# VectorE's order per job in the MLP of a hybrid decoder block: the job's weight panels split first, its slot evicted second

## What is computed

```
v = rms_norm(h, g_ffn[i])
up = causal_dwconv(v @ w_up[i], w_conv_ffn[i], b_conv_ffn[i])   # w_up 1024 x 6144, 3 taps along the sequence
gate = up[..., :D_FF]                                           # D_FF = 3072
val = up[..., D_FF:]
h = h + (jax.nn.gelu(gate) * val) @ w_down[i]                   # w_down 3072 x 1024
```

## Time and profile before

| | |
|---|---|
| median of 3 runs | 2380.67 us (2378.57 to 2381.3) |
| profiled execution, span | 2378.7 us (its own time beside the span is not listed) |
| TensorE busy | 2294.0 us, 96% of the span, 9968 matmuls |
| VectorE busy | 1281.4 us, 54% |
| ScalarE busy | 814.1 us, 34% |
| DMA | 142.47 MB, mean 60 GB/s |
| chain that ended last | PE 86%, DVE 5%, ACT 5%, issue 2%, DMA 1% |

### The profile page before, as it was taken

How to read it: one execution, slowest core, us unless ns; L and a number is a source line. 1 busy time by engine, 2 the same in 40 slices (tenths; PEclk the granted TensorE clock), 3 DMA queues, 4 the chain that set the end, 5 groups by cost and what they waited for, 6 DMA issues and landing times.

```text
span 2378.7 us, 27030 instructions
## 1 busy us (share of the span) xinstructions
PE 2294.0 (96%) x9968; PEld 1882.6 (79%) x9968; DVE 1281.4 (54%) x1532; ACT 814.1 (34%) x971; POOL 0.2 (0%) x4
## 2 busy tenths in 40 slices
PE   7999999999999999999889999999999999999995
PEld 5787888888888888887767778888888888888784
DVE  6774466524653355545677735654255624554445
ACT  5663333202331133333545624332133302333432
POOL 0000000000000000000000000000000000000000
PEclk9999999999999999999999999999999999999997
DMA  3113111111111111123121031111111111111123
GB/s 126 45 45 121 39 54 54 45 54 45 53 46 50 49 46 53 45 82 114 54 98 50 31 133 45 53 45 53 45 53 46 50 49 45 54 45 54 54 66 110
DMA packets 69715, 142.47 MB, mean 60 GB/s; under 512 B 7504, under 2 KB 7632, under 8 KB 69584
## 3 DMA queue, kind: packets, MB, share of 16 engines
q1 hardware_dynamic: 69584, 140.68, 18.3%
HBM read 132.26 MB, written 8.39 MB: 59 GB/s over the span
## 4 chain that ended last, share of the span: by engine, by line
PE 86%; DVE 5%; ACT 5%; issue 2%; DMA 1%; SPq 0%; ACTq 0%; DVEq 0%
PE slot L355 85%; DMA raw<-panels 1%; DVE H L770 1%; DVE H L834 1%; PE slot L388 1%; ACT L481 1%; PE slot L404 1%; DVE wlo L671 0%; ACT whi L472 0%; ACT L567 0%; DVE H L832 0%; ACT H L567 0%; DVE H L789 0%; ACT Uhi L504 0%; ACT H L569 0%
## 5 line engine op out<-in xcount | busy, mean ns | idle before, releaser
L355 PE MATMUL slot<-Uhi,whi 128*128 128x512 f32 x2176 | 677.1, 392 | 29.1 <-DVE wlo L671 21.6
L355 PE MATMUL slot<-Ulo,whi 128*128 128x512 f32 x2176 | 672.9, 390 | 0.0
L355 PE MATMUL slot<-Uhi,wlo 128*128 128x512 f32 x2176 | 672.0, 390 | 0.0
L472 ACT ACTIVATE whi<-raw 128x512 fp32r<-128x512 f32 x428 | 247.3, 623 | 979.4 <-PE slot L355 926.8
L355 PEld LDWEIGHTS slot<-Uhi,whi 128*128 128x128 f32 x2176 | 409.6, 189 | 122.6 <-DVE Ulo L704 22.6
L355 PEld LDWEIGHTS slot<-Ulo,whi 128*128 128x128 f32 x2176 | 410.4, 189 | 86.0
L355 PEld LDWEIGHTS slot<-Uhi,wlo 128*128 128x128 f32 x2176 | 410.2, 189 | 85.7
L355 PE MATMUL slot<-Ylo,whi 128*128 128x512 f32 x1024 | 316.7, 390 | 0.0
L671 DVE TENSOR_TENSOR wlo<-raw,whi 128x512 fp32r<-128x512 f32 x428 | 276.3, 686 | 29.9 <-ACT whi L472 26.9
L901 DVE TENSOR_TENSOR H<-slot,H 128x1024 f32<-128x1024 f32 x48 | 58.8, 1225 | 334.1 <-PE slot L355 334.1
L680 DVE TENSOR_TENSOR WG<-slot,RS 128x1024 f32<-128x1024 f32 x72 | 88.2, 1225 | 268.4 <-PE slot L355 267.9
(11 more groups left out here) (146 smaller groups left out, 1463.7 us busy)
## 6 DMA issues: line engine op xcount, KB each, us to landing
raw<-panels SPq DMA_DIRECT2D x432, 256.0 KB, 2.7
XN<-xT SPq DMA_DIRECT2D x8, 1024.0 KB, 10.2
H<-xT SPq DMA_DIRECT2D x8, 1024.0 KB, 10.0
outT<-H SPq DMA_DIRECT2D x16, 512.0 KB, 3.0
WG<-pT SPq DMA_DIRECT2D x2, 512.0 KB, 4.8
WV<-pT SPq DMA_DIRECT2D x2, 512.0 KB, 6.3
par<-parameters SPq DMA_DIRECT2D x1, 136.0 KB, 2.2
```

What stands on the lines that cost most here:

```text
L355: mm = pe.matmul(ps[:, t], stat[n % RING][:, w], mov[:, t], start=first and k == 0 and i == 0, stop=last and k == ks - 1 and i == len(pass ...
L472: nc.scalar.activation(whi[n % RING][:], raw[n % RING][:], ACT.Copy).then_inc(panel_hi, 1)
```

## The change

In the MLP VectorE's `refill` moves ahead of the eviction of the same job. For gate and val jobs it moves ahead of `scaled_out` (and so ahead of `f_lo(j - 1)` and the halo copy); for down jobs it moves ahead of the addition to H, but stays behind the wait for the job. The same instructions run, with the same waits and the same semaphores. ScalarE, TensorE and SyncE are unchanged.

```diff
                         v.tensor_copy(work[:, 0:HALO_FFN], halo_c[:, i:i + HALO_FFN])
                         if (j, stream) == (0, 0):
                             dve.wait_ge(dve_chain, ffn_scale)
+                        refill(jj, bp_c)
                         scaled_out(b, jj, work[:, HALO_FFN:HALO_FFN + BLOCK], bj, bs)
                         if stream == 0 and j:
                             f_lo(j - 1)
                         v.tensor_copy(halo_c[:, i:i + HALO_FFN], work[:, BLOCK:BLOCK + HALO_FFN]).then_inc(ready, 1)
-                        refill(jj, bp_c)
                         dve.wait_ge(summed, pairs + j + 1)
...
                     for m in range(DT):
                         jj = JOBS[("down", 0, m)]
                         dve.wait_ge(jobs_done, bj + jj + 1)
+                        refill(jj, bp_c)
                         v.tensor_tensor(H[:, m, :], slot[jj % RING][:], H[:, m, :], ALU.add
                                         ).then_inc(slot_free[jj % RING], 1)
-                        refill(jj, bp_c)
```

## The result

The changed kernel is slower by about 0.4%: 2389.07 us in the median of four runs (2388.53 to 2389.6) against 2380.18 of the kernel before beside it, a ratio of 1.0042 with a 95% interval of 1.0028 to 1.0057. Run again beside the experiments it gave 2388.56 against 2378.61, ratio 1.0041 (1.0027 to 1.0054). (The ratios are those on record; the quotient of the first two medians is 1.0037.) The forecast was 2390.8 (2386.5 to 2394.8), from six stalls of 1.69 us.

The account below looks back on a forecast made before the run. The MLP was taken as bound by unbroken TensorE matmuls, with 0.35 us slack at each chunk's last hidden tile. Six stalls of 1.69 us, 10.1 us, added to the median 2380.67 gave 2390.8 us, range 2386.5 to 2394.8.

Parts of the forecast that it names:

- six stalls of 1.69 us: TensorE waits in down 0 at each of six chunk ends for the last hidden tile's low part; 10.1 us in all.
- What bounds the kernel, and the slack: MLP is unbroken TensorE matmuls; down 0's tile k = 7 is ready only 0.35 us before it is due.
- The delay: Val job's eviction starts 1.85 to 1.93 us later, 1.89 taken: 0.64 waiting for ScalarE's split plus 1.21 to 1.29 for VectorE's.
- The loss per stall: At down 0 of each chunk: tile ready at 463.77, due at 462.23, plus 0.15 restart, 1.69 us.
- the restart: TensorE's first matmul after a stall must be restarted, costing 0.14 to 0.15 us on top of the lateness.
- The end of the range with only VectorE's work in it: If splits need not wait for ScalarE: delay 1.29 us, stall 1.09 per chunk, sum 6.5 us.
- Gate jobs, down jobs, panels, slots at no cost: Later gate evictions, additions to H and slot releases, and earlier panel splits, stay within cover in the MLP: cost and gain 0.
- First pair: At a block's start, val 0's splits hold its eviction until about 307.0; val 1 needs the panels at 311.4: cost 0.
- No stall: Rival: slack at tile k = 7 absorbs the delay and TensorE goes on; 2380.7 us, 5%, really faster 1%.
- The falling clock: Rival: TensorE's clock drops after each chunk-end stall, 1.7 us more each, sum 20 us, 2401 us; 4%.
- The adding up of delays: Rival: per-job delay above about 3.2 us makes ScalarE's next split late; 21.5 us, 2402 us; 3%.
- What was to be seen: Profile sign: six TensorE waits for the low part (line 868), 1.5 to 1.8 us each, in the MLP; clock 1.00 there.

Follow-up runs that it names:

- the two dummies: Kernel before, with two unread 128x512 VectorE multiplications added ahead of val 7's eviction, no split moved; 2384.78 us against 2378.61, ratio 1.0024.
- the single split: Kernel before, with one of val 7's two VectorE splits moved ahead of its eviction, the other left behind the halo copy; 2385.87 us against 2378.94, ratio 1.0028.
- the kernel without val 7: Changed kernel, but val 7 of each chunk keeps the order of before (evict, halo copy, splits); 2379.63 us against 2378.94, ratio 1.0001.
- the one with the down jobs alone: Kernel before, with the splits moved ahead only in down jobs, gate and val jobs as before; 2380.03 us against 2378.94, ratio 1.0002.

## Why the prediction was right

- *What bounds the kernel, and the slack.* Right. The page said that VectorE is half idle; the number that decided stands only in the timelines, 0.35 us at one tile of one job per chunk.
- *The delay.* 1.85 to 1.93 was forecast and 1.89 taken; 1.88 was measured. Both parts were shown alone: the splits by the two dummies (1.21), the wait for ScalarE by the single split (0.66 when the work is halved, 0.67 in the changed kernel, 0.64 in the sum).
- *The loss per stall.* 1.69 forecast, 1.69 and 1.70 measured at the first chunk, the restart among it: the tile came 1.52 us late (462.46 where 460.94 was due), so the restart was 0.17 where 0.15 had been taken. The six stalls together are 10.2 us against 10.1. The MLPs grew by only 9.6 to 9.8, since the profile of before has more in breaks between the chunks (0.49 + 0.30 us) than those of the changed kernel (0.21 and 0.39). The end of the range with only VectorE's work in it (6.5 us) is in effect the two dummies' 6.2.
- *The point forecast* of 2390.8 was 1.7 above the measured 2389.07. Part is that 2380.67 was the median of three runs of a kernel whose other medians here are 2380.18, 2378.94 and 2378.61. In the differences of the medians, 8.9 and 10.0 were measured against 10.1; they differ by 1.1 us between themselves, so that the second comes so near is in part luck.
- *Gate jobs, down jobs, panels, slots at no cost.* Right, shown by the kernel without val 7 and by the one with the down jobs alone. How long a delay per job would have to be before it adds up was not tried; the cover is read from rows. ScalarE's split of val 7 now has 1.34 us of cover, forecast 1.4:

```profile
451.62 1.15 ACT L472 ACTIVATE whi<-raw 128x512 fp32r<-128x512 f32 x2 [1.34 <-PE slot L355]
```

- *First pair.* The splits of val 0 end 19.06 us after the stat job's start (305.70 - 286.64), where 307.0 - 287.93 = 19.07 was forecast.
- *The rivals.* No stall was excluded by all six waits. The falling clock did not come at 1.4 us of idle time, but it was a real danger: 2.3 us more and it came at each of the six. My price for it, 1.7 us a time, was near the 1.4 to 1.65 of five of them; the other cost 2.85. The adding up of delays did not occur.
- *What was to be seen.* I had named waits of 1.5 to 1.8 us for TensorE; the view says 1.4. This is the way of counting, not the size of the loss.

## What to carry to other kernels

Where an engine waits nowhere, look for the least slack among what it consumes: work moved ahead of the head of that chain is paid in full beyond it, however idle the engines are on average. Count with the moved work what it waits for itself; here over a third of the loss (0.66 of 1.69 us) was another engine's wait that used to be hidden. An order can be harmless for 23 jobs and costly for one: a swap is to be judged at the end of a loop, where no further job lies between the last product and its reader.

## What the runs showed of the hardware

- An operand that is ready only 0.01 us ahead of its due time already breaks the flow of matmuls: 0.16 to 0.19 us lost at each of six chunk ends. With 0.35 us ahead nothing was lost.
- TensorE's granted clock stayed at 1.00 behind stalls of 1.4 us, and fell to its lower level at each of six stalls of 3.7 us; the fall cost 1.4 to 1.65 us at five of them and 2.85 at the sixth.
